# Winograd's form of Strassen's product in the first MLP matmul, and weight splits by half units, in a hybrid decoder step on one core

## What is computed

```python
x  = x + g1 * merge_branches(o_att, bgate * yc, ga, gb, w_att_out, w_conv_out, w_o)
h2 = rms_norm(x, rms_g2) * (1 + sc2) + sh2
x  = x + g2 * (jnp.square(jax.nn.relu(h2 @ w_mlp1)) @ w_mlp2)   # D_MODEL 1024, D_FF 4096
```

## Time and profile before

| | us |
|---|---|
| median of 3 runs (1683.91 to 1685.92) | 1685.39 |
| the profiled execution's own time | 1683.69 |
| its span, first to last instruction | 1681.9 |
| PE busy / weight loads busy | 1643.0 / 1529.7 |
| DVE / ACT / POOL busy | 869.5 / 374.5 / 598.3 |

### The profile page before, as it was taken

One profiled execution on the slowest core, in us unless ns is written; L12 is line 12 of the kernel. 1 busy time (PEld: TensorE's weight loads), 2 busy tenths in 40 slices (PEclk: granted clock), 3 DMA queues, 4 the chain that ended last, 5 costly groups with the idle time before them and its releaser, 6 DMA issues.

```text
span 1681.9 us, 29994 instructions
## 1 busy us (share of the span) xinstructions
PE 1643.0 (98%) x11976; PEld 1529.7 (91%) x11976; DVE 869.5 (52%) x1365; ACT 374.5 (22%) x718; POOL 598.3 (36%) x344
## 2 busy tenths in 40 slices
PE   7999999999999999999999999999999999999999
PEld 5898788878788788899999999999999999999998
DVE  5554364564454454338743865464555545454543
ACT  6344222222222222231111521020202011110200
POOL 0344143343343333314243243343343344343342
PEclk9999999999999999999999999999999999999999
DMA  9112446556666666325321011111111111111112
GB/s 380 41 51 88 154 154 224 203 199 227 191 213 227 209 225 235 139 104 205 128 102 51 26 60 41 51 50 40 51 51 38 51 50 39 51 51 39 51 41 101
DMA packets 71931, 194.63 MB, mean 116 GB/s; under 512 B 8017, under 2 KB 8146, under 8 KB 71794
## 3 DMA queue, kind: packets, MB, share of 16 engines
q1 hardware_dynamic: 67394, 178.62, 30.6%
q10 hardware_dynamic: 4400, 14.10, 2.2%
HBM read 174.26 MB, written 18.42 MB: 115 GB/s over the span
## 4 chain that ended last, share of the span: by engine, by line
PE 91%; DVE 2%; POOL 2%; ACT 1%; issue 1%; DMA 1%; SPq 1%; ACTq 0%; POOLq 0%; DVEq 0%
PE bank L657 77%; PE bank L807 2%; PE bank L782 2%; PE bank L795 2%; PE bank L831 2%; PE bank L855 1%; PE bank L687 1%; POOL wl L592 1%; DMA pre<-in_weights 1%; POOL wh L590 1%; DVE act L1319 1%; DMA ring<-in_cache_v 0%; PE bank L707 0%; PE bank L842 0%; DVE qsqL L1323 0%
## 5 line engine op out<-in xcount | busy, mean ns | idle before, releaser
L590 POOL TENSOR_TENSOR wh<-raw,zero 128x1024 fp32r<-128x1024 f32 x84 | 160.3, 1908 | 628.5 <-PE bank L657 628.5
L592 POOL TENSOR_TENSOR wl<-raw,wh 128x1024 fp32r<-128x1024 f32 x114 | 281.1, 2466 | 110.8 <-ACT wh L1091 104.3
L657 PE MATMUL bank<-hH,wh 128*128 128x352 f32 x832 | 276.5, 332 | 1.2 <-POOL wl L592 0.8
L657 PE MATMUL bank<-hL,wh 128*128 128x352 f32 x832 | 267.4, 321 | 0.0
L657 PE MATMUL bank<-hH,wl 128*128 128x352 f32 x832 | 266.9, 321 | 0.0
L657 PE MATMUL bank<-h2H,wh 128*128 128x352 f32 x768 | 248.6, 324 | 1.3 <-POOL wl L592 1.3
L657 PE MATMUL bank<-hidH,wh 128*128 128x352 f32 x768 | 247.7, 323 | 0.0
L657 PE MATMUL bank<-hidH,wl 128*128 128x352 f32 x768 | 246.3, 321 | 0.0
L657 PE MATMUL bank<-h2H,wl 128*128 128x352 f32 x768 | 246.2, 321 | 0.0
L657 PE MATMUL bank<-hidL,wh 128*128 128x352 f32 x768 | 246.1, 320 | 0.0
L657 PE MATMUL bank<-h2L,wh 128*128 128x352 f32 x768 | 246.0, 320 | 0.0
(11 more groups left out here) (179 smaller groups left out, 2570.9 us busy)
## 6 DMA issues: line engine op xcount, KB each, us to landing
raw<-in_weights SPq DMA_DIRECT2D x152, 512.0 KB, 3.5
ring<-in_cache_k SPq DMA_DIRECT2D x128, 256.0 KB, 4.0
ring<-in_cache_v SPq DMA_DIRECT2D x128, 256.0 KB, 3.7
pre<-in_weights SPq DMA_DIRECT2D x16, 512.0 KB, 16.2
gate_scratch<-gt ACTq DMA_DIRECT2D x14, 528.0 KB, 3.4
act<-gate_scratch SPq DMA_DIRECT2D x14, 528.0 KB, 4.7
xt<-in_xT SPq DMA_DIRECT2D x8, 528.0 KB, 7.3
act<-in_xT SPq DMA_DIRECT2D x8, 528.0 KB, 4.7
```

What stands on the lines that cost most here:

```text
L590: mark(pool.tensor_tensor(wh[u % 2][:, :], src[:, :], zero[:, 0:1].to_broadcast([P, 1024]), ALU.add))
L592: pool.tensor_tensor(wl[u % 2][:, :], src[:, :], wh[u % 2][:, :].bitcast(F32), ALU.subtract)\
L657: mm = pe.matmul(out, x, y, start=n == 0, stop=n == end)
```

## The change

The MLP goes by 16 pairs p of two hidden blocks instead of 8 groups of four, in the order m1(0), m1(1), m2(0), m1(2), m2(1), .... Pairs 0 and 1 compute m1 as before, in 6 groups of 24 matmuls of 352 columns. From pair 2 on m1(p) is Strassen's scheme in Winograd's form: the 1024 x 256 weights are quarters A11, A12 (first unit), A21, A22 (second unit), `h2` is quarters B11..B22 (4 blocks of channels by half of the tokens, 528 columns), and there are seven products of quarters. A product is two groups of 4 x 3 matmuls of 264 columns, into two banks: 24 matmuls. The sums are S1 = A21 + A22, S2 = S1 - A11, S3 = A11 - A21, S4 = A12 - S2 for the weights (POOL, for each pair, four operations of 512 columns) and T1 to T4 for the tokens (DVE, once, in 15 steps, each a tensor_tensor of 4 x 528 = 2112 columns; ACT rounds the four high parts). m2(p) is 8 output blocks x 3 chunks = 24 groups of 2 x 3 = 6 matmuls of 352 columns.

Weights are split by halves (512 columns): ACT makes all high parts of the MLP, POOL the low parts; a half may be split when the half four places before it is used up. The MLP uses all eight banks. Seven products are combined on DVE, which adds five of them from PSUM to what is in `part` and makes two further sums; ACT copies two products. DVE squares the four tiles and writes their low parts, ACT their high parts.

```diff
+PLAIN = 2
+PRODUCTS = (Product("A11", "B11", "a"), Product("A12", "B21", "d"), Product("S2", "T2", "d"), Product("S1", "T1", "a"),
+            Product("S3", "T3", "d"), Product("S4", "B22", "d"), Product("A22", "T4", "d"))
...
+            elif kind == "m1":
+                for j, product in enumerate(PRODUCTS):
+                    at += at % 2
+                    self.add("s", (), (p, j), product.eng, (at % 8, at % 8 + 1))
+                    at += 2
             else:
-                for q in range(4):
-                    for m in (0, 1):
-                        for c in range(NCH):
-                            self.add("m2", self.m2_unit[f, q], (f, q, m, c), "d", b5)
+                for d in range(DB):
+                    for c in range(NCH):
+                        self.add("m2", self.m2_unit[p, d // 4], (p, d, c), "d", (at % 8,))
+                        at += 1
+    def half_free(self, i):
+        return self.half_end[i - 4] if i >= 4 else self.end[self.mlp0 - 2 + i // 2]
...
+T_AT = {GROUP_OF["m1", 0, 0, 0] + 3 + n: n for n in range(9)}
+T_AT.update({GROUP_OF["m2", 0, d, 2]: n for d, n in ((0, 9), (2, 10), (4, 11), (6, 12))})
+T_AT.update({GROUP_OF["s", PLAIN, 0]: 13, GROUP_OF["s", PLAIN, 3]: 14})
...
@@ GpSimd, before half S2 is split @@
+            def weight_sums(p):
+                pool.wait_ge(S[f"raw_in{j % NRAW}"], 16 * (j // NRAW + 1))
...
+                mark(pool.tensor_tensor(s3[:, :], a11, a21, ALU.subtract))
+                mark(pool.tensor_tensor(a21, a21, a22, ALU.add))
+                pool.wait_ge(S["split"], PLAN.mlp0 + first + 2)
+                mark(pool.tensor_tensor(a11, a21, a11, ALU.subtract))
+                pool.tensor_tensor(a12, a12, a11, ALU.subtract).then_inc(S["weight_sums"], 1)
...
@@ TensorE @@
+            def winograd(g):
+                split_done(i)
+                if p == PLAIN and PRODUCTS[j].tokens[0] == "T":
+                    pe.wait_ge(S["t_lo"], int(PRODUCTS[j].tokens[1]))
+                release(g)
+                for t in (0, 1):
+                    cols = slice(SUB * t, SUB * t + SUB)
+                    mm = three(bank[GROUPS[g].bank + t][:, 0:SUB],
+                               [(w[:, kt * P:kt * P + P], wlow[:, kt * P:kt * P + P], y[:, kt, cols], yl[:, kt, cols]) for kt in range(4)])
...
@@ ScalarE @@
             for g in range(MLP0, len(GROUPS)):
+                if GROUPS[g].kind == "m1":
+                    plain(g, g - MLP0)
+                elif GROUPS[g].kind == "s":
+                    p, j = GROUPS[g].c
+                    if j in TILES:
+                        tile_hi(g)
+                    else:
+                        if PRODUCTS[j].eng == "a":
+                            product_copy(g)
+                half_high(g)
+                if g in T_HIGH:
+                    t_high(T_HIGH[g])
...
@@ VectorE @@
+            def product_add(g, at, other):
+                tt(part[at][:, :, :], two_banks(g), part[other][:, :, :], ALU.add).then_inc(S["bank_dve"], 1)
+            def tile_square(g):
+                stt(t[:, :, :], t[:, :, :], 0.0, t[:, :, :], ALU.max, ALU.mult).then_inc(S["hid_sq"], 1)
+            def tile_lo(p, j):
+                tt(hid_tile(hidL, p, j), part[TILES[j].at][:, :, :], f(hid_tile(hidH, p, j)), ALU.subtract).then_inc(S["hid_lo"], 1)
+            def add_m2(g):
+                if c < 2:
+                    stt(x, ps[:, 0:CH], gate, x, ALU.mult, ALU.add).then_inc(S["bank_dve"], 1)
+                    return
+                mark(tt(y_samp[:, d, :], ps[:, LASTP:CH], y_samp[:, d, :], ALU.add))
+                stt(x, ps[:, 0:LASTP], gate, x, ALU.mult, ALU.add).then_inc(S["bank_dve"], 1)
+                if p == PAIRS - 1:
+                    mark(tt(by_sequence(y_samp[:, d, :]), by_sequence(y_samp[:, d, :]), per_sequence(40 + d), ALU.mult))
+                    tt(act8[:, d, samp], act8[:, d, samp], y_samp[:, d, :], ALU.add).then_inc(S["y_ready"], 1)
```

More of the change, by code:

```diff
@@ L37 @@
 NMOD = 6
-FFG = FF // 512
+PAIRS = FF // 256
+HALF = T // 2
+SUB = T // 4
 GRP = 4
@@ L89 @@
 SQ_USERS = list(SQ_NTH)
+PLAIN = 2
+Product = namedtuple("Product", "weights tokens eng")
+PRODUCTS = (Product("A11", "B11", "a"), Product("A12", "B21", "d"), Product("S2", "T2", "d"), Product("S1", "T1", "a"),
+            Product("S3", "T3", "d"), Product("S4", "B22", "d"), Product("A22", "T4", "d"))
 def mlp_order():
     out = [("m1", 0)]
-    for f in range(1, FFG):
-        out += [("m1", f), ("m2", f - 1)]
-    return out + [("m2", FFG - 1)]
+    for p in range(1, PAIRS):
+        out += [("m1", p), ("m2", p - 1)]
+    return out + [("m2", PAIRS - 1)]
+Half = namedtuple("Half", "u what pair")
 class Plan:
@@ L117, in __init__ @@
         self.m1_unit, self.m2_unit = {}, {}
-        for kind, f in mlp_order():
-            for q in range(4):
-                (self.m1_unit if kind == "m1" else self.m2_unit)[f, q] = len(self.where)
-                self.where.append((W_M1 if kind == "m1" else W_M2) + 4 * f + q)
+        self.halves, self.half_at, self.half_end = [], {}, {}
+        for kind, p in mlp_order():
+            for q in (0, 1):
+                u = len(self.where)
+                (self.m1_unit if kind == "m1" else self.m2_unit)[p, q] = u
+                self.where.append((W_M1 if kind == "m1" else W_M2) + 2 * p + q)
+                if kind == "m2" or p < PLAIN:
+                    for h in (0, 1):
+                        self.half(kind, u, h, p, q)
+            if kind == "m1" and p >= PLAIN:
+                for j, product in enumerate(PRODUCTS):
+                    first = product.weights in ("A11", "A12", "S2", "S4")
+                    self.half("s", self.m1_unit[p, 0 if first else 1], product.weights, p, j)
         self.groups = []
@@ L127, in __init__, with half @@
         self.build()
+    def half(self, kind, u, what, p, q):
+        self.half_at[(kind, p, q, what) if kind != "s" else (kind, p, q)] = len(self.halves)
+        self.halves.append(Half(u, what, p))
     def add(self, kind, u, c, eng, banks):
         n = len(self.groups)
-        bank = banks[(n - self.base) % len(banks)]
-        self.groups.append(Group(kind, u, c, bank, eng, self.counts[eng] + 1, self.held.get(bank)))
+        both = banks if kind == "s" else (banks[(n - self.base) % len(banks)],)
+        before = sorted({self.held[x] for x in both if x in self.held})
+        self.groups.append(Group(kind, u, c, both[0], eng, self.counts[eng] + 1, before))
         self.counts[eng] += 1
-        self.held[bank] = (eng, self.counts[eng])
+        for x in both:
+            self.held[x] = (eng, self.counts[eng])
         for x in u if isinstance(u, tuple) else (u,):
@@ L192, with plain_unit, splits_of, tiles_before @@
 GROUPS = PLAN.groups
-BY_ACT = [*range(14, 42), PLAN.mlp0, PLAN.mlp0 + 1]
+GROUP_OF = {(x.kind, *x.c): n for n, x in enumerate(GROUPS) if x.kind in ("m1", "s", "m2")}
+HALVES = PLAN.halves
+BY_ACT = [*range(14, 42)]
+def plain_unit(i):
+    return HALVES[i].what in (0, 1) and HALVES[i].u in [PLAN.m1_unit[p, q] for p in range(PLAIN) for q in (0, 1)]
+def splits_of(u):
+    if u < PLAN.mlp0:
+        return u + 1
+    return PLAN.mlp0 + max(i + 1 for i, x in enumerate(HALVES) if x.u == u)
+def tiles_before(p):
+    return 6 * min(p, PLAIN) + 4 * max(p - PLAIN, 0)
+Tile = namedtuple("Tile", "n block half at")
+TILES = {1: Tile(0, 0, 0, 1), 4: Tile(1, 1, 1, 2), 5: Tile(2, 0, 1, 1), 6: Tile(3, 1, 0, 0)}
+T_AT = {GROUP_OF["m1", 0, 0, 0] + 3 + n: n for n in range(9)}
+T_AT.update({GROUP_OF["m2", 0, d, 2]: n for d, n in ((0, 9), (2, 10), (4, 11), (6, 12))})
+T_AT.update({GROUP_OF["s", PLAIN, 0]: 13, GROUP_OF["s", PLAIN, 3]: 14})
+T_HIGH = {g: {2: 0, 4: 1, 8: 2, 13: 3}[n] for g, n in T_AT.items() if n in (2, 4, 8, 13)}
 Step = namedtuple("Step", "p i c n final")
@@ L452, in program, with two_banks, hid_tile, place_of @@
         MERGE0, WO0, MLP0 = (PLAN.phase[n][0] for n in ("merge", "wo", "mlp"))
+        def two_banks(g):
+            return psum[:, GROUPS[g].bank:GROUPS[g].bank + 2, 0:SUB]
+        def hid_tile(t, p, j):
+            at = HALF * TILES[j].half
+            return t[p % 2][:, TILES[j].block, at:at + HALF].rearrange("p (a n) -> p a n", a=2)
+        def place_of(i, n=512):
+            at = slice(512 * (i % 2), 512 * (i % 2) + n)
+            return wh[i // 2 % 2][:, at], wl[i // 2 % 2][:, at]
+        def source_of(i, n=512):
+            x = HALVES[i]
+            if x.what == "S3":
+                return s3[:, 0:n]
+            at = 512 if x.what in (1, "A12", "S4", "A22") else 0
+            return raw[RAW_OF["dense", x.u] % NRAW][:, at:at + n]
+        def quarter(which, n, half):
+            return (h2H, h2L)[which][:, 4 * n:4 * n + 4, HALF * half:HALF * half + HALF]
         def gate_place(x, part):
@@ L645, in release @@
             def release(g):
-                if GROUPS[g].before:
-                    eng, at = GROUPS[g].before
+                for eng, at in GROUPS[g].before:
```

(35 more changed lines are left out.)

268 lines of the change are left out of this document (231 added, 37 removed).

## The result

The changed kernel takes 1662.86 us (median of 4 runs, 1661.66 to 1663.52) against 1685.12 us before (4 runs). The ratio is 0.9868, with a 95% interval of 0.9853 to 0.9884: 22.3 us, or 1.3%, less. The forecast was 1657 us, 28.2 us less.

The account below looks back on a forecast made before the run. PE's 4464 MLP matmuls without a wait were taken as the bound. Products -39.5, opening +10.6 and end +0.7 gave -28.2 us; from 1683.69 that is 1655.5, plus 1.7 for the median: 1657 us, range 1643 to 1676.

Parts of the forecast that it names:

- The products: PE's m1 from pair 2 on: 22.90 us a pair becomes 20.08, 14 pairs give -39.5 us, ends -45.4 and -26.6.
- I take 0.1195: Price in us of a 264-column matmul on PE, load just under the stream; ends 0.117 and 0.125.
- a little of either in each pair: Rival for the products: pace 0.123 us or 0.6 us of waiting a pair, +8 us, 1665 us; chance 14%.
- taken at nothing: m2's smaller groups of 6 matmuls on PE cost 0; 10 ns lost on each of 192 more groups would be 2 us.
- The steady state: Work of DVE, POOL, ACT and loads after the opening is hidden by PE: cost 0, 2.5 us spare at the narrowest.
- 7 x 1.27: In each pair's products, seven POOL operations of 1.27 us block DVE: 10.6 us of work becomes 19.5, against PE's 20.1.
- The opening: Start of the MLP: late third-unit split and DVE's queue of token steps make PE wait, +10.6 us; ends +2 and +20.
- The end: After the last matmul: small operations some 0.3 us and closer output blocks +0.4 us, together +0.7 us.
- The opening is covered: Rival: POOL's operations fall beside DVE's PSUM ones, so the opening loses 2 us in place of 10.6: 1648 us; chance 15%.
- The load of weights is the pace of these matmuls: Rival: each product matmul costs 0.159 us, a pair 26.7 us, 3.8 more than before: 1750 us; chance 6%.
- the short formula: Rival: the skill's N / 2.4 + 2.5 ns holds for 264 columns, 112.5 ns, gain 56 us: 1640 us; chance 3%.
- The splits come late in each product: Rival: DVE's lag outgrows the 2.5 us spare, products take 3.5 us in place of 2.87, +62 us: 1719 us; chance 5%.

Follow-up runs that it names:

- the table: Changed kernel, products of pairs 4 to 9 narrowed to between 256 and 128 columns a matmul: a pair takes 20.39 us at 264, 18.84 at 240, 18.70 at 128.
- three plain pairs: Changed kernel with a third pair computed without products and the 15 token steps spread: 1658.38 us; with ACT's third-unit high part also made earlier, 1653.38 us.
- the late high parts: Changed kernel with ACT rounding the high parts of T1 and T2 one group later, behind its relu and square of the next m1 group: 1657.75 us.
- the same edit: ACT makes the third unit's high part before m1(0)'s third group: 1663.95 us on the changed kernel, 1653.38 us with three plain pairs and spread steps.

## Why the prediction was right, point by point

**The bound and the direction: right.** PE bounds the MLP before and after, and the products' saving is the only gain.

**The products: right in kind, 4.4 us too much.** The step that was mis-sized is the price of a matmul of 264 columns, "I take 0.1195". Measured is 20.39 / 168 = 0.1214. Within the stated ends, but not at the value taken: it lies halfway to the 0.123 of the rival "a little of either in each pair". The excess lies evenly on the matmuls of a product, none of it at the products' starts: the distances are 0.119 to 0.124 us at each of the 24 places. Near the floor the price no longer follows the columns alone. Between 264 and 240 columns the table's slope is 9.3 / 24 = 0.39 ns a column, where 352 and 512 columns gave 0.45. Why is open; with half as many columns of weights to load all but a quarter of the excess stays (0.08 of 0.31 us a pair). The bound by the load was right: 0.111, beside the 0.110 and 0.117 of the nearest rows.

**m2's groups of 6: "taken at nothing", cost 0.9 us.** The bound given was 2 us.

**The steady state: right.** No wait of PE in 647 us. DVE is less loaded than I had it: 9.35 us in a pair's products and 17.3 in m2 in this stretch, where I had 19.5 and 13.2; some of a pair's squares and low parts run in the m2 pass behind it. Over many pairs, from 1300 to 1640 us, it is busy for 214.2 of 340 us, 27.3 a pair where I had 32.7; that is 63% of the time, below my 70 to 85%. The next two rows are the stretches of a pair's products and of the m2 pass behind it.

```profile
1112.20:1132.60 20.40, 20.40 (x170) 20.40 (x169) 9.35 (x13) 5.86 (x10) 8.70 (x6) 1.00 0.17 53
1132.60:1155.50 22.90, 22.90 (x146) 22.90 (x145) 17.26 (x35) 4.23 (x7) 11.59 (x9) 1.00 0.14 47
```

The error is in "7 x 1.27": POOL's and DVE's operations meet less often than that. With my 23.8 us of DVE work a pair unblocked, POOL costs it 3.5 us, not 9.

**The opening: right in place and mechanism, +12.3 where I had +10.6, but with other parts.** The wait for the split was 3.9 (I had 3.5) and the wait at the ninth group 5.4 (5). DVE, busy for 91% of the time from 965 to 1045 (I had over 90), came to that eviction at 1007.5 (1006), but by a different sum. POOL blocked `rsq` and `hidL` for 8.3 us in place of 10.2, and the two idle pieces behind ACT, 4.8 us, were in no term. The Trainium skill's rule (SBUF — State Buffer, SBUF: two separate sides), that one of the two engines has the shared ports for a whole instruction, held as in the earlier trace rows:

```profile
968.06 2.67 DVE L1857 TENSOR_TENSOR rsq<-rel 128x352 f32<-128x352 f32 x1
970.76 2.58 DVE L1860 TENSOR_TENSOR hidL<-rsq,hidH 128x352 fp32r<-128x352 f32 x1
```

But steps of 2.35 us were blocked only three times, by 0.6 to 1.1 us. The wait I expected later, some 3 us for T4's low part before product 6, did not come: pair 2's products took 20.38 us. It was close. DVE's row for that low part ends at 1042.3, and product 6 starts at 1043.0:

```profile
1038.89 3.44 DVE L1989 TENSOR_TENSOR h2L<-t4f,h2H 128x2112 fp32r<-128x2112 f32 x1
```

In the place of that wait stands what I left out, 3.8 us at 1.2 GHz with the two waits. The two errors nearly cancelled, and that the sum came out so near is luck.

**The end: +0.7 forecast, +0.1 measured.** From the last matmul to the last output's issue it is 1656.75 - 1655.26 = 1.49 us, against 1.39.

**The rivals.** "The opening is covered" is what three plain pairs bring about, and only with the split moved too. "The load of weights is the pace of these matmuls" is excluded by the table, and "the short formula" as well: it gives 0.1125 us where 0.1214 was measured. "The splits come late in each product" never happened. "A little of either in each pair" is half true: no waits, but about half of its dearer pace.

**The sum.** -28.2 us was forecast and -22.3 measured. The products are 4.4 of the difference, m2's groups 0.9, the opening 1.7; the end gives 0.6 back, and m1(0)'s earlier end 0.2. The 0.3 us that are left are less than the runs of one kernel differ by. The result of 1662.9 is nearer to that last rival's 1665 than to 1657.

## What to carry to other kernels

A scheme that moves fewer columns in all, but in more and narrower matmuls (here 168 of 264 for 144 of 352), pays by columns only down to the floor, which here fits the time of one weight load; price the narrow matmul from the floor that short matmuls show in the trace, and take it a little above the line of the wide ones. What such a scheme needs once, at its start, is worth a table of each engine's work against PE's time there, with every engine's order of waits: here 15 operations of 2.35 us, with ACT's four, gave back 8 of the products' 35 us, 5 of them by ACT's order alone, and starting the scheme one pair later with the steps spread, at a price of 2.5, made room for them. A fix of one wait is worth nothing as long as the engine behind the next one is the late one: the same edit won 0 and then 5 us.

## What the runs showed of the hardware

In the changed kernel PE worked 3 to 4 us at 1.2 GHz after its wait of 3.9 us and again after that of 5.4 us, which cost 3.8 us together. With a wait of 2.9 us, in the run without the products and in the one without the token steps, the clock fell as well. With the wait of 0.83 us before, and those of at most 0.7 us in m2(0) with the late high parts, it stayed at 2.4 GHz. A matmul with a load of 128 columns of fp32r weights never came below 0.111 us on average over a pair's products: 0.1121 with 240 columns to move, 0.1113 with 128. DVE's operations with one input from PSUM kept their time while POOL worked: the 27 adds of 528 columns that overlapped a POOL operation took 0.707 us on average, the other 43 took 0.703. Of the 56 squares of 528 columns, which read SBUF alone, the 29 that overlapped one took 1.77 us, the other 27 took 0.71.
